# A delta-rule recurrence on one core: levels that stay on their partitions, fewer and larger products, one falling exponential

## The reference

```python
def step(S, inp):
    r_t, w_t, a_t, b_t, k_t, v_t = inp
    sa = jnp.einsum('bhvk,bhk->bhv', S, a_t)
    S = S * w_t[:, :, None, :] + sa[..., None] * b_t[:, :, None, :] + v_t[..., None] * k_t[:, :, None, :]
    return S, jnp.einsum('bhvk,bhk->bhv', S, r_t)
```

## Time and profile before

| | |
|---|---|
| median of three runs | 2594.62 us |
| profiled execution, time of the program | 2594.5 us |
| its span, first to last instruction | 2592.7 us |
| PE busy | 2253.1 us (87%) in 19954 matmuls |
| PE weight loads | 1492.5 us (58%), 19954 |
| DVE, ACT, POOL busy | 1159.0, 707.5, 392.0 us |
| mean granted TensorE clock | 0.941 |
| instructions in the program | 49039 |

### The profile page before, as it was taken

The page is one execution under the profiler, slowest core; times in us unless marked ns, Lnnn a source line. Parts: engine busy times, 40 slices in busy tenths (PEclk is TensorE's granted clock), DMA queues, the critical chain, the costliest instruction groups (busy, mean ns, idle before and its releaser), DMA issues. The chain is left out here.

```text
span 2592.7 us, 49039 instructions
## 1 busy us (share of the span) xinstructions
PE 2253.1 (87%) x19954; PEld 1492.5 (58%) x19954; DVE 1159.0 (45%) x2561; ACT 707.5 (27%) x1666; POOL 392.0 (15%) x465
## 2 busy tenths in 40 slices
PE   6999989887789998899889679999888878897785
PEld 3444455547754444466556568877657767554453
DVE  3877765575542114532212563244675542522113
ACT  2011155464441002132222120024454430222220
POOL 0000000044520001132222000000133400222210
PEclk8999999999999998999999889999889999899998
DMA  9455401210016103699988733313210033999994
GB/s 379 195 211 238 168 33 43 79 46 5 4 52 259 73 1 126 263 384 388 372 348 319 297 143 113 115 67 98 98 40 4 4 128 129 355 414 390 382 377 180
DMA packets 80368, 474.39 MB, mean 183 GB/s; under 512 B 17296, under 2 KB 29200, under 8 KB 51728
## 3 DMA queue, kind: packets, MB, share of 16 engines
q1 hardware_dynamic: 55280, 419.82, 41.3%
q0 software_dynamic: 24864, 51.43, 5.2%
HBM read 439.99 MB, written 61.08 MB: 193 GB/s over the span
## 5 line engine op out<-in xcount | busy, mean ns | idle before, releaser
L2883 PE MATMUL xp_psG<-moe_ring,rt_xt 128*64 128x256 f32 (+1 forms) x2048 | 324.5, 402 | 42.5 <-DMA moe_ring<-in_moe 41.9
L2883 PEld LDWEIGHTS xp_psG<-moe_ring,rt_xt 128*64 128x64 f32 (+1 forms) x2048 | 225.4, 161 | 119.6 <-issue 48.2
L599 PE MATMUL win_ps<-h,win_ring 128*128 128x512 f32 x512 | 226.2, 600 | 5.4 <-PEq L292 5.4
L659 DVE SCALAR_TENSOR_TENSOR mod_acc<-ada_ring,cv_silu,mod_acc 128x512 f32<-128x512 f32 x280 | 197.9, 748 | 10.8 <-issue 0.4
L3140 DVE TENSOR_TENSOR rt_sg<-rt_sg,xp_psG 128x128 f32<-128x128 f32 x84 | 24.2, 288 | 332.3 <-ACT rt_sg L2957 332.3
L599 PEld LDWEIGHTS win_ps<-h,win_ring 128*128 128x128 f32 x512 | 97.0, 192 | 125.6 <-issue 125.6
L2904 PE MATMUL xp_psY<-moe_ring,rt_aT 128*64 128x512 f32 (+1 forms) x512 | 162.1, 602 | 4.0 <-DVE rt_aT L3147 4.0
L2192 PE MATMUL sc_ps<-sc_NT,sc_XI 64*64 64x64 f32 x2560 | 112.9, 235 | 23.3 <-issue 18.9
L1274 POOL MEMSET ml_w<- 128x1536 f32 x4 | 5.4, 1376 | 764.9 <-POOLq L973 764.9
L2187 PE MATMUL sc_ps<-sc_XI,sc_NT 64*64 64x64 f32 x2048 | 100.7, 226 | 22.1 <-issue 16.6
L2073 DVE TENSOR_TENSOR sc_XI<-sc_ps,cst 128x256 f32<-128x256 f32 x160 | 67.5, 422 | 107.9 <-PE sc_ps L2192 107.0
(11 more groups left out here) (537 smaller groups left out, 4293.4 us busy)
## 6 DMA issues: line engine op xcount, KB each, us to landing
moe_ring<-in_moe SPq DMA_DIRECT2D x128, 1536.0 KB, 14.3
ada_ring<-in_ada SPq DMA_DIRECT2D x22, 2048.0 KB, 15.1
win_ring<-in_win SPq DMA_DIRECT2D x20, 2048.0 KB, 7.8
cb_yg<-y_rows SPq DMA_DIRECT2D x16, 1024.0 KB, 11.6
mg_ring<-in_mg SPq DMA_DIRECT2D x16, 768.0 KB, 4.4
mg_wo<-in_wo SPq DMA_DIRECT2D x2, 4096.0 KB, 14.5
pr<-y_rows SPq DMA_DIRECT2D x8, 1024.0 KB, 18.4
ml_gate_ring<-in_mg SPq DMA_DIRECT2D x12, 512.0 KB, 3.7
```

Source lines behind the costliest of these rows:

```text
L599: last = pe.matmul(ps[:, n % NB, first(n):T], ring[:, j % 2, c, m * P:(m + 1) * P], h[:, c, first(n):T], start=c == 0, stop=c == KD - 1)
L659: last = dve.scalar_tensor_tensor(out=acc[:, a % 2, s], in0=aring[:, a % 3, c], scalar=weight, in1=acc[:, a % 2, s], op0=ALU.mult, op1=ALU ...
L2883: last = pe.matmul(psG[at:at + m, u % 2, 0:2 * P].rearrange("p (q n) -> p q n", q=2), xt[:, u % 2, c, at:at + m], ring[:, slot, c:2 * KD:K ...
```

## The change

The change edits only `stage_rwkv_scan`.

- Exponentials: `ex` and `wl` go. `rise` is the rising one; `fall`, three buffers of L + 1 columns, is one falling exponential of all cumulated sums, and its readers take columns 1-d to 1-d+L, d to d+L, or the last or first one.
- `matrices`: one product a head with 64 x 128 weights (b and k side by side) in place of two; the results of both heads lie on the same partitions: b rows on 0 to 63, k rows on 64 to 127. `psA2`, X0 and M's level part are on partitions 0 to 63 for all heads, the even heads in one PSUM bank and the odd ones in another; `matrices` waits for the token copy of the step before between its two groups.
- `level`: no `place`, no semaphore `across`, no wait inside a level; all results stay on partitions r to r + 64.
- Turning: four 128 x 128 transposes per direction in place of 16 products; each direction turns its own keys and signals by itself; ACT copies them in one piece. Values are copied in two pieces of 64 x 512, to partitions 64 to 127 for all heads, and all of them ahead of `matrices(d, 0)`.
- PE's order: both `matrices` ahead of both `corrections`; `corrections(d, n)` waits for the first factor of step n + 1 of its direction and no longer for the token copy. The last step has no state product, sum or decay.

```diff
-                    act.activation(ex[d][:, 2], incl, ACT.Exp, scale=DECAY)
-                    act.activation(ex[d][:, 0], incl, ACT.Exp, scale=-DECAY)
-                    act.activation(ex[d][:, 1], excl, ACT.Exp, scale=-DECAY)
-                    act.activation(wl[n % 3][d][:], total, ACT.Exp, scale=-DECAY).then_inc(sem[d]["exps"].sem, 1)
+                    act.activation(rise[d][:], sums[:, :, 1 - d:1 - d + L], ACT.Exp, scale=DECAY)
+                    act.activation(fall[n % 3][d][:], sums, ACT.Exp, scale=-DECAY).then_inc(sem[d]["exps"].sem, 1)
...
-                        act.activation(at[HD:P, 0:HEADS:2], src[r:r + HD, :, 0:HD], ACT.Copy)
-                        last = act.activation(at[0:HD, 1:HEADS:2], src[r:r + HD, :, HD:P], ACT.Copy)
+                        last = act.activation(at[HD:P].rearrange("p h n -> p (h n)"), src[r:r + HD], ACT.Copy)
...
-                    dve.copy_predicated(X0[:, d], level_mask(d, 0).bitcast(U32), psA2[d]).then_inc(sem[d]["xi"].sem, 1)
+                    for o in range(2):
+                        last = dve.copy_predicated(X0[d][:, o:HEADS:2], level_mask(d, 0)[0:HD].bitcast(U32), psA2[d][o])
+                    last.then_inc(sem[d]["xi"].sem, 1)
...
-                        o = h % 2
-                        for a, q in enumerate((r, HD - r)):
-                            pe.matmul(psA[d][q:q + HD, o, hp], hat[n % 2][d][r:r + HD, hp, a],
-                                      ra[n % 2][d][r:r + HD, hp].rearrange("p a n -> p (a n)"), start=True, stop=True)
+                        pe.matmul(psA[d][:, h % 2, hp], hat[n % 2][d][r:r + HD, hp].rearrange("p a n -> p (a n)"),
+                                  ra[n % 2][d][r:r + HD, hp].rearrange("p a n -> p (a n)"), start=True, stop=True)
+                    if n:
+                        w(pe, d, "tok", n - 1)
...
-                        return HD - r if hp >= KC // 2 and m % 2 else r
...
+                        if m == 0:
+                            return M[n % 2][d][0:HD, r // HD, hp, L:P], X0[d][:, 2 * hp + r // HD]
+                        return NT[d][r:r + HD, hp], XI[d][r:r + HD, hp]
...
-                            last = backward(hp + KC // 2, psWT[d][:, hp + KC // 2])
-                        last.then_inc(sem[d]["across"].sem, 1)
+                            backward(hp + KC // 2, psWT[d][:, hp + KC // 2])
                         between(d, n, m)
-                        w(pe, d, "across", n, m + 1)
...
                         for hp in range(KC):
-                            for o, e in ((0, d), (1, 1 - d)):
-                                r = o * HD
-                                for a, q in enumerate((r, HD - r)):
-                                    last = pe.matmul(psBK[e][o][q:q + HD, hp], hat[n % 2][e][r:r + HD, hp, a],
-                                                     k.cst("ident")[r:r + HD, r:r + HD], start=True, stop=True)
+                            last = pe.transpose(psBK[d][:, hp * P:(hp + 1) * P],
+                                                hat[n % 2][d][:, hp].rearrange("p a n -> p (a n)"), k.cst("ident"))
+                        last.then_inc(sem[d]["turned"].sem, 1)
...
                     w(pe, d, "inv", n)
-                    w(pe, d, "tok", n)
+                    if n + 1 < NST:
+                        w(pe, d, "xi", n + 1)
+                    else:
+                        w(pe, d, "tok", n)
...
+                    if n + 1 < NST:
+                        for d in range(2):
+                            matrices(d, n + 1)
                     for d in range(2):
-                        if n + 1 < NST:
-                            matrices(d, n + 1)
                         corrections(d, n)
...
+                for j in range(NV):
+                    values(j)
+                pe.wait_ge(values_out.sem, values_out.at(NV))
```

More of the change, by code:

```diff
@@ L1852, in stage_rwkv_scan @@
         S2 = sb("S2", [P, KC, L])
-        ex = sb("ex", [P, 3, KC, L])
+        rise = sb("rise", [P, KC, L])
+        fall = [sb(f"fall{b}", [P, KC, L + 1]) for b in range(3)]
         ra = [sb("ra", [P, KC, 2, L]),
@@ L1860, in stage_rwkv_scan @@
         XI = sb("XI", [P, KC, L])
-        X0 = ctx.enter_context(nc.sbuf_tensor(f"sc_X0{l}", [P, 2, KC, L], F32))
+        X0 = [pn[0:HD, NK_T + 2 + d].rearrange("p (h n) -> p h n", h=HEADS) for d in range(2)]
         bk = sb("bk", [P, HEADS, L])
@@ L1876, in stage_rwkv_scan @@
         psWT = [half(d, 1, 0) for d in range(2)]
-        psA2 = [half(d, 3, 1) for d in range(2)]
-        psV = [ps[d][:, 2].rearrange("p (c n) -> p c n", c=KC) for d in range(2)]
-        psBK = [[half(d, 2, o) for o in range(2)] for d in range(2)]
+        psA2 = [[half(d, 3 - o, 1)[0:HD] for o in range(2)] for d in range(2)]
+        psV = [ps[d][:, 2] for d in range(2)]
+        psBK = [ps[d][:, 2] for d in range(2)]
         psI = [ps[d][:, 0:2, 0:2 * L].rearrange("p b (c n) -> p b c n", c=KC // 2) for d in range(2)]
@@ L1937, in token_major @@
                     w(act, d, "turned", n)
-                    for o in range(2):
-                        last = act.activation(bk[d][:, o:HEADS:2], psBK[d][o], ACT.Copy)
-                    last.then_inc(sem[d]["tok"].sem, 1)
+                    act.activation(bk[d][:].rearrange("p h n -> p (h n)"), psBK[d], ACT.Copy).then_inc(sem[d]["tok"].sem, 1)
                 def right_side(d, n):
@@ L2111, in step @@
                     if n + 1 < NST:
-                        for d in range(2):
-                            first_factor(d, n + 1)
-                            masks(d, n + 1)
-                    for d in range(2):
-                        add_products(d, n)
-                    dve.drain()
-                    for d in range(2):
-                        decay(d, n)
-                        if n + 1 < NST:
+                        first_factor(0, n + 1)
+                        masks(0, n + 1)
+                        first_factor(1, n + 1)
+                        masks(1, n + 1)
+                    if n + 1 < NST:
+                        for d in range(2):
+                            add_products(d, n)
+                        dve.drain()
+                        for d in range(2):
+                            decay(d, n)
                             factor(d, n + 1, 1)
-                    dve.drain()
+                        dve.drain()
                 for d in range(2):
@@ L2145, in values @@
                     for hp in range(KC):
-                        last = pe.transpose(psV[j % 2][:, hp], pr[:, V_T + hp, j * P:(j + 1) * P], k.cst("ident"))
+                        last = pe.transpose(psV[j % 2][:, hp * P:(hp + 1) * P], pr[:, V_T + hp, j * P:(j + 1) * P], k.cst("ident"))
                     last.then_inc(values_ps.sem, 1)
```

63 lines of the change are left out of this document (24 added, 39 removed).

## The result

The changed kernel takes 2607.96 us (median of 9 runs, 2601.86 to 2613.6); the kernel before took 2593.35 us beside it (9 runs, 2586.23 to 2602.57). The ratio is 1.0055, 95% interval 1.0037 to 1.0073: slower by 14 us (10 to 19). The forecast was 2605 us, slower.

A forecast was written before the change was run, and what follows sets the result against it. PE was taken as bound by instruction fetch, about 4.0 us per 256 instructions. Steps +5.4, first levels +2.0, last step -1.4, stage start +2.0 and clock +3 made +11 on the median 2594.62, about 2605 us; range 2583 to 2630.

The forecast's parts named there:

- The step: Recurrence step: 22.5 us full, 21.1 without rows; twelve steps 264.4 against 259.0, so +5.4 us.
- The stream that was put together from bursts of the old trace: PE's work in a full step, summed from record burst times: 19.5 us after the change, 5.0 more than before.
- The fetch: PE in the recurrence steps outruns its instruction fetch, about 4.0 us per block of 256 instructions.
- The rule that was weighed: Skill text on PE's instruction fetch: refill of 16 KiB blocks of 256 instructions, cost mostly hidden; the 1.6 us gap disagrees.
- The 0.3 us a step left to the gaps: Fetch gaps in PE's step almost vanish; 0.3 us a step stays, bounds 0 and 2.4.
- The rival in which they stay on top: Fetch gaps in PE's steps keep 0.5 us a block despite the slower stream: +31 us, 2636, chance 0.13.
- The switches: Array shape changes around transposes and in matrices: seven new ones a step at 0.13, 0.9 us, bounds 0 and 1.1.
- The drain rule: Skill text on array packing: changing the tiling mode drains TensorE; without it the step would be 0.9 us less.
- The wait for the second first factor: PE before corrections(1) waits 1.3 us for VectorE's second first factor, starting at x+4.5 after matrices(0) starts at x.
- First levels and start: Stage start to matrices: first levels +0.5 us, +1.5 in layer 1, together +2.0; late start in layer 1 another +2.0.
- Last step: End of each recurrence stage, without state products: 26.9 us against 27.6, so -1.4 us for both layers.
- The clock: Recurrence stages: most stretches at 1.2 GHz go; those left cost 0.43 of their length, taken as +3 us.

The follow-up runs named there:

- e1: Kernel before with one part of the change, keys turned by 8 transposes a step instead of 32 products: 2565.88 us, ratio 0.9878.
- e8: Kernel before with one edit, every level product from rows r to columns r, two array quadrants instead of four: 2600.57 us, ratio 1.003.
- e9: Kernel before with both the transposes in place of turning products and every level product on two quadrants: 2594.72 us, ratio 1.0005.
- e4: Changed kernel with psA2 in one bank again, corrections no longer waiting for the next first factor, matrices not for the token copy: 2604.04 us, ratio 1.003.
- e11: Kernel before with the transposes in place of turning products, the same kernel as e1 timed again: 2571.5 us, ratio 0.9907.

## Why the prediction was right

**The step.** Forecast 22.5 and 21.1 us, measured 22.39 and 20.98 (one of four 21.20); twelve steps 264.4, measured 263.3. The stream that was put together from bursts of the old trace holds: 32 level records at 0.0585 a pair, no pair closer, 616 records, `matrices(0)` to level 0 7.26 us where 7.0 was forecast, the rest 15.1 for 15.5.

**The fetch.** That PE's gaps of 1.0 to 2.1 us were the fetch of instructions, about 4.0 us a block of 256, rested on the trace alone. e1, e8 and e9 show it together: with fewer instructions the kernel before gains 26 to 32 us in the stages, of which the clock is the smaller part, with a longer stream it loses its gaps and only some 8 us of time, with both the gain is gone. 4.0 us a block holds to 2% in three step forms. The forecast's 22.1 for the old step had stretches at 1.2 GHz in it; at full clock it is 21.7, 3.9 us a block, which changes nothing in the argument. The rule that was weighed (the Trainium skill, "Runtime: NRT & Kernel Launch", Instruction fetch mechanics: refill mostly hidden) does not hold for the stream of the kernel before, as its 27.9 us of gaps and e1 show. The 0.3 us a step left to the gaps was 0 in both layers. The rival in which they stay on top (2636) fell with the empty list of waits.

**The switches.** In the rows of the step four transposes stand between 64x64 products. From 674.76 to 675.73 PE starts four records of 64x64, the four transposes and four records of 64x64 again. That is 0.97 us, where their own time is 4 x 0.109 + 2 x 0.117 = 0.67 (0.117 is two pairs of records at 0.0585): 0.30 for both switches, 0.15 each, where 2 x 0.13 was taken. The 64x128 groups take 1.09 (657.11 to 658.20) for 0.93, the 64x64 group between them 0.62 (658.20 to 658.82) for 0.47: 0.16, 0.15 and 0.16. The seven come to 2 x 0.30 + 0.47 = 1.07 us, forecast 0.9 with 1.1 as the bound. The drain rule (the Trainium skill, "TensorEngine Tiling (Array Packing)", Key Properties) agrees in sign.

**The wait for the second first factor.** Forecast 1.3 us, and `corrections(1)` at x+4.5. It came at 661.74, x+4.6, after 0.85 us of waiting: the last record of `corrections(0)` started at 660.42 + 0.63 - 0.22 = 660.83, and 0.06 later the next could have. The switches in `matrices`, which the forecast had added to the step without putting them in this stretch, delayed `matrices(1)` and `corrections(0)` by as much as the wait is shorter; hence level 0 at x+7.3 instead of 7.0, and next to no error in the sum. The second error is the worth of the wait: without it (e4) the step is 0.42 shorter, not 0.7 or 0.85, since the copy of u takes 0.4 of it back.

**First levels and start.** Two stretches of each layer, from the stage's start to the second `matrices` and the last step up to the next stage, first of the kernel before, then of the changed one:

```profile
564.30:590.53 26.23, 18.92 (x592) 17.03 (x593) 17.04 (x40) 16.09 (x52) 15.61 (x24) 0.81 0.01 2
723.47:751.30 27.83, 23.06 (x832) 21.56 (x832) 11.85 (x27) 9.77 (x28) 8.40 (x13) 0.92 0.02 4
1916.40:1945.90 29.50, 20.32 (x592) 18.28 (x593) 16.43 (x40) 15.63 (x50) 15.31 (x24) 0.73 0.01 3
2071.86:2100.20 28.34, 22.32 (x832) 20.70 (x832) 12.36 (x27) 9.85 (x28) 8.32 (x13) 0.94 0.02 4
```

```profile
563.20:589.95 26.75, 23.42 (x504) 20.84 (x505) 17.82 (x42) 13.12 (x32) 16.22 (x24) 0.82 0.01 2
724.27:751.20 26.93, 25.06 (x713) 23.37 (x713) 11.01 (x26) 9.93 (x26) 8.13 (x13) 1.00 0.02 4
1915.50:1948.56 33.06, 27.46 (x505) 24.68 (x505) 17.37 (x42) 13.08 (x32) 15.09 (x24) 0.71 0.01 2
2077.53:2104.50 26.97, 25.10 (x713) 23.42 (x713) 11.03 (x26) 9.94 (x26) 8.13 (x13) 1.00 0.02 4
```

The first stretch is +0.5 in layer 0, as forecast (nothing at the start, +0.5 for the levels), and +3.6 in layer 1 (2.0 + 1.5 forecast).

**Last step.** -0.9 and -1.4, together -2.3; forecast -1.4. The terms of the first pair of traces are then 4.3 + 0.5 + 3.6 - 2.3 = +6.1, the measured 6.0.

**The clock.** Here the sum was wrong: +3 was taken, and none of the twelve steps has a stretch at 1.2 GHz. The reason given was that PE streams in nearly nine tenths of a step. No step of e1 has such a stretch either, with PE busy in 101.4 of 120.0 us of layer 0 and gaps of up to 1.8 us (before, 104.8 of 132.9 us); what brought the lower clock in the kernel before stays open. Its steps hold an estimated 14 us of it in the first trace; at equal clock the change costs that much more in the steps than the 4.3 us measured. The forecast had this in it, since it set a new step at full clock against an old one with its losses. The clock of the stages is 0.97 and 0.95, and what is missing lies ahead of the second `matrices` (0.82 and 0.71 in the rows just shown), where it lay before too (0.81 and 0.73). Without this term the forecast for the stages is +8.0; measured +6.0 and +12.4 between the two pairs of traces.

**The total.** 2605 against 2607.96. That it comes so near is luck in part: the stages give 6 to 12 of the 14 us. The rest lies outside of them, 4.4 us between the first traces and 6.8 between the second, in stages that the change doesn't touch, where untouched code varied by 16 us over all traces. Whether the changed kernel really is slower there was not tried. The same is open for the 8 us of e8.

**Which parts of the change cost.** By the ratios from the kernel before: transposes -0.0122 (or -0.0093, e11), two quadrants on top +0.0127 (e9), all else +0.005, 13 us, in which is the wait of e4 (about 4 us, intervals overlapping). The remaining 9 are not separated. The first `matrices` behind all copies, the 64x128 products with their switches, the exponentials and the larger copies are in them; that the exponentials and copies cost nothing, as forecast, no run tried alone.

## What to carry to other kernels

When an engine's idle time is marked with no semaphore, recurs once per fixed number of instructions, and vanishes where the stream is slow, the count of instructions is the limit: then fewer and larger instructions pay, and extra streaming costs little until it nears the length of the fetch. The two limits combine about as the larger one, so one must price each edit at the pace that the others leave: here the transposes were worth 24 to 32 us and the simpler layout cost some 8, each alone, and together they cancelled. Take from a change of many parts the one that moves the limit and run it alone. Compare steps at the same granted clock, and trace a kernel twice before reading 6 us into it.

## What the runs showed of the hardware

- PE needs about 4.0 us for 256 of its instructions when they are small: 4.0, 3.95 and 4.0 us a block at 5.5, 5.06 and 4.56 blocks a step (3.9 and 4.0 in the steps with rows of before and e1 that ran at full clock). Where the stream is shorter than that, gaps of 1 to 2 us stand in it; where it is longer, almost none (e8: 3.8 us in layer 0, the changed kernel: none).
- Single steps of a kernel paced by fetch vary (e1: 18.8 to 20.8 us in layer 0), those of one paced by its stream repeat to 0.01 us (changed kernel, layer 0). The sum over the stages repeated to 1.4 us for e1 and to 0.6 for the changed kernel, and differed by 5.8 in the kernel before, where the clock differed too.
- The kernel before had its stages at a mean clock of 0.94 and 0.88, in the second trace 0.95 and 0.93; e8, with the same instructions but a closed stream, 0.97 and 0.96. But e1 had 0.97 and 0.95 with gaps of up to 1.8 us, and 1.00 in all twelve steps, so gaps alone do not bring the lower clock.
- A switch between 64x64 products and 64x128 products or 128x128 transposes cost 0.15 us: a group of transposes between 64x64 products took 0.30 us more than its records, both switches together.
